# Attention and scan projections of a two-block transformer: fp32 products replaced by three rounded products each, the decay of the keys by one, attention's output projection in two halves

## What is computed

```python
def fox_attention(h, w_in, b_f, g_q, g_k, w_out):        # 16 heads of 64
    q, k, v, f_logit = split(h @ w_in)
    q, k = rms_norm_2(q per head, g_q), rms_norm_2(k per head, g_k)
    cum = cumsum(log_sigmoid(f_logit + b_f))              # per head, over tokens
    s = q @ k.T * 64 ** -0.5 + cum[query] - cum[key]      # causal softmax over keys
    return softmax(mask(s)) @ v @ w_out

def hgrn2_recurrence(h, w_in, b_f, lower_bound, g_o, w_out):   # 8 heads of 128
    q, f_logit, v, g = split(h @ w_in)
    f = lower_bound + (1 - lower_bound) * sigmoid(f_logit + b_f)
    k, q, log_f = 1 - f, silu(q), log(f)
    # per chunk: b = cumsum(log_f)
    # scores[t, s] = sum_k q[t,k] k[s,k] exp(b[t,k] - b[s,k]);  o = scores @ v + (q exp(b)) @ state
    return (rms_norm_2(o, g_o) * silu(g)) @ w_out
```

## Time and profile before

| | us |
|---|---|
| median of 3 runs | 2997.9 |
| lowest and highest | 2996.49 and 3000.87 |
| the profiled execution | 2997.82 |
| its span, first to last instruction | 2996.0 |
| attention stage, first to last job's matmul | about 1428.9 to 1702.9 |
| scan stage, first to last job's matmul | about 2231.0 to 2470.9 |

### The profile page before, as it was taken

One profiled execution on the slowest core, in us unless ns is written; L12 is line 12 of the kernel. 1 busy time (PEld: TensorE's weight loads), 2 busy tenths in 40 slices (PEclk: granted clock), 3 DMA queues, 4 the chain that ended last, 5 costly groups with the idle time before them and its releaser, 6 DMA issues.

```text
span 2996.0 us, 45640 instructions
## 1 busy us (share of the span) xinstructions
PE 2750.9 (92%) x18786; PEld 1951.7 (65%) x18786; DVE 1439.4 (48%) x3248; ACT 777.4 (26%) x1479; POOL 0.2 (0%) x4
## 2 busy tenths in 40 slices
PE   5999887998999997999999999999989989999998
PEld 4998776998999876899766743333346765333332
DVE  3885773787786574654233223333332613333333
ACT  3332352433332253433232111111112332111110
POOL 0000000000000000000000000000000000000000
PEclk9999898999999998999988899999999989999999
DMA  8775420576575420444111169999972124999997
GB/s 341 265 278 228 154 71 32 212 269 235 221 283 202 167 80 7 163 175 183 71 43 57 57 267 427 428 427 428 428 306 98 64 78 186 429 426 427 428 427 300
DMA packets 71735, 701.56 MB, mean 234 GB/s; under 512 B 8672, under 2 KB 11104, under 8 KB 11360
## 3 DMA queue, kind: packets, MB, share of 16 engines
q1 hardware_dynamic: 71520, 698.54, 58.3%
HBM read 697.46 MB, written 1.05 MB: 233 GB/s over the span
## 4 chain that ended last, share of the span: by engine, by line
PE 76%; DVE 10%; DMA 8%; ACT 4%; issue 2%; SPq 0%; DVEq 0%; ACTq 0%
PE ps L790 14%; PE ps L1245 13%; DMA ring<-slabs 7%; PE ps L1266 7%; PE ps L1461 6%; PE ps L1462 6%; PE ps L1463 6%; PE ps L1283 5%; PE ps L783 4%; DVE acc L716 3%; PE ps L1026 2%; PE ps L1413 1%; PE ps L994 1%; PE ps L1215 1%; DVE ring_parts L3005 1%
## 5 line engine op out<-in xcount | busy, mean ns | idle before, releaser
L1461 PE MATMUL ps<-arena_parts 128*128 128x256 f32 x2112 | 606.1, 287 | 24.1 <-DVE arena_parts L3089 24.1
L1462 PE MATMUL ps<-arena_parts 128*128 128x256 f32 x2112 | 601.3, 285 | 0.0
L1463 PE MATMUL ps<-arena_parts,ring_parts 128*128 128x256 f32 x2112 | 601.2, 285 | 0.0
L1245 PE MATMUL ps<-ring,arena 128*64 128x512 f32 x2048 | 470.3, 602 | 5.2 <-ACT arena L1966 4.9
L790 PE MATMUL ps<-h,ring 128*128 128x256 f32 (+1 forms) x1664 | 407.3, 404 | 27.0 <-DVE h L2470 10.0
L1461 PEld LDWEIGHTS ps<-arena_parts 128*128 128x128 f32 x2112 | 409.4, 194 | 25.5 <-issue 25.3
L1462 PEld LDWEIGHTS ps<-arena_parts 128*128 128x128 f32 x2112 | 409.6, 194 | 0.2
L1463 PEld LDWEIGHTS ps<-arena_parts,ring_parts 128*128 128x128 f32 x2112 | 409.1, 194 | 0.0
L790 PEld LDWEIGHTS ps<-h,ring 128*128 128x128 f32 x1664 | 328.6, 200 | 88.3 <-issue 10.9
L3005 DVE TENSOR_TENSOR ring_parts<-ring,arena_parts 128x2048 fp32r<-128x2048 f32 x132 | 299.1, 2288 | 75.7 <-ACT arena_parts L1622 75.7
L1622 ACT CAST arena_parts<-ring 128x2048 fp32r<-128x2048 f32 x132 | 249.4, 1906 | 300.6 <-DMA ring<-slabs 284.4
(11 more groups left out here) (391 smaller groups left out, 2450.3 us busy)
## 6 DMA issues: line engine op xcount, KB each, us to landing
ring<-slabs SPq DMA_DIRECT2D x192, 2048.0 KB, 14.9
ring<-slabs SPq DMA_DIRECT2D x278, 1024.0 KB, 5.0
x<-xT SPq DMA_DIRECT2D x1, 1024.0 KB, 8.8
outT<-x SPq DMA_DIRECT2D x1, 1024.0 KB, 4.7
constants<-const SPq DMA_DIRECT2D x1, 1004.5 KB, 6.6
vectors<-vec SPq DMA_DIRECT2D x1, 747.5 KB, 4.6
ring<-slabs SPq DMA_DIRECT2D x2, 128.0 KB, 3.6
arena<-pos SPq DMA_DIRECT2D x1, 128.0 KB, 7.2
```

What stands on the lines that cost most here:

```text
L1245: mm = nc.tensor.matmul(ps[W * hh:W * hh + W, e % 2, :], xe[:, e % 2, 4 * k + c], wt[:, c], start=(k == 0 and c == 0), stop=(k == 1 and c ...
L1461: nc.tensor.matmul(out, w_hi, v_hi, start=start, stop=False, skip_group_check=True)
L1462: nc.tensor.matmul(out, w_hi, v_lo, start=False, stop=False, skip_group_check=True)
L1463: return nc.tensor.matmul(out, w_lo, v_hi, start=False, stop=stop, skip_group_check=True)
```

## The change

In both stages all projections become three products of float32r (`thirds`). For this each slab is followed in the plan by an entry `high`, which is not loaded but takes a ring slot: ScalarE writes the rounded slab there (`high_part`), VectorE writes the rest over the slab itself (`low_part`). The ring so holds four slabs in place of eight. `h` is split as well, by ScalarE and VectorE, at the entry of each stage and before the output projections. The scan's output norm goes in four pairs of tiles. The cumulated gates of the keys are held as a high and a low part on 48 partitions and added by one float32r product for a head. Half of the attention's output projection (the first four k) runs as 8 `half` jobs within units 18 to 24, each added to `x` at once; the `out` jobs do the other four k. In the scan all value jobs come before the gate jobs.

```diff
 def slab_plan(stages):
-            out += [("foxin", 4 * part + g, "pe") for g in range(4) for part in range(3)]
-            out += [("foxout", s, "pe") for s in range(4)]
+            out += with_low([("foxin", 4 * part + g, "pe") for g in range(4) for part in range(3)]
+                            + [("foxout", s, "pe") for s in range(4)])
+            out += with_low([("hgin", s, "pe") for s in range(16)] + [("hgout", s, "pe") for s in range(4)])
+def with_low(slabs):
+    return [s for one in slabs for s in (one, ("high",) + one[1:])]
-HG_LAST = tuple(range(2, 18, 2)) + (29, 30, 31, 32, 26, 28, 34, 36)
+HG_LAST = tuple(range(2, 18, 2)) + (25, 26, 27, 28, 30, 32, 34, 36)
-            17: ("j27", "t3"), 20: ("t4",), 21: ("t5",)}
+            17: ("j27", "t3"), 18: ("h0", "h1"), 19: ("h2",), 20: ("t4", "h3"), 21: ("t5", "h4"), 22: ("h5",), 23: ("h6",),
+            24: ("h7",)}
+FOX_HIGH = {1: 8, 4: 9, 6: 10, 9: 11, 11: 12, 13: 13, 15: 14, 18: 15}
-        out += value(0) + value(1) + gate(0) + value(2) + gate(4)
+        out += value(0) + value(1) + value(2) + gate(0) + gate(4)
...
 run_jobs, wide jobs (value jobs alike)
+                                mm = thirds(bank(b, n), w_hi[:, k, c0:c0 + P], w_lo[:, k, c0:c0 + P], rhs[0][:, k], v_lo,
+                                            k == ks[0], k == ks[-1])
 attention, scores
-                            mm = nc.tensor.matmul(o, ident[0:FOXH, head:head + 1].to_broadcast([FOXH, qn]),
-                                                  view(NCUM, T2)[0:FOXH, 0:keys], start=False, stop=True)
+                            mm = nc.tensor.matmul(o, part(PICK, FOXH)[64 * e:64 * e + 48, head:head + 1].to_broadcast([48, qn]),
+                                                  part(NCUM, T2)[64 * e:64 * e + 48, 0:keys], start=False, stop=True)
...
 ScalarE
+            def high_part(i):
+                slab_here(act, i)
+                if i + 1 >= RING:
+                    name, value = free[i + 1 - RING]
+                    act.wait_ge(s[name], value)
+                nc.scalar.copy(low_view(i + 1), slab_view(i)).then_inc(s["p_hi"], 1)
 entry of either stage
+                    for j in range(2):
+                        high_part(nth_slab(st, slab, j))
                     norm_root(q, n_norm, n)
+                    for j in range(2, 4):
+                        high_part(nth_slab(st, slab, j))
+                    for k in range(KC):
+                        act.wait_ge(s["h_mul"], n_h + k + 1)
+                        mark(nc.scalar.copy((fox_hi if st[0] == "fox" else sq_parts)[:, k], h[:, k]), q, "h_hi", k)
 attention stage: high(4), fox_forget, high(5), three value_in and root, high(6), fox_keys, root(3), four square, high(7),
 units with high(FOX_HIGH[n_unit]) last in the unit
 scan stage
                 for i in range(16):
                     take(i)
+                    if i >= 3 and i % 2:
+                        high(i // 2 + 3)
 high(11) after the logs; high(12) to high(15) after takes 26, 27, 28, 30; high(16), high(17) before the gate's silu
+                for p in range(4):
+                    await_("act", q, "hon0", 2 * p + 1)
+                    v = sq[:, 2 * p:2 * p + 2]
+                    mark(nc.scalar.activation(v, v, ACT.Exp, scale=-0.5), q, "hon", p)
...
 VectorE
+            def low_part(i):
+                dve.wait_ge(s["p_hi"], halved_at[i] + 1)
+                nc.vector.tensor_tensor(low_view(i), slab_view(i), low_view(i + 1).bitcast(F32), ALU.subtract)\
+                    .then_inc(s["p_lo"], 1)
 entry: low_part of slabs 0 and 1, norm with the subtraction of tile k-2 behind multiply k, low_part of slabs 2 and 3
 attention stage: low parts behind fox_forget, three fox_norm, fox_low_keys, four fox_in (before the first softmax_max)
 scan stage
+                for n in range(4, 8):
+                    low(n)
                 for c in range(KC):
+                    if c in (2, 4, 6):
+                        low(7 + c // 2)
                     dve.wait_ge(s["proj_act"], act_before(q) + KC + c + 1)
 low(11) after the cumulated sums; 12, 13 at the end of tile 1; 14, 15 after levels 1 and 3 of tile 2; 16, 17 at its end
```

More of the change, by code:

```diff
@@ L240, in stage_jobs @@
             out += [("fv", (g, t), 3 * g + 2, 0, "act") for t in range(3)]
+        out += [("half", c, 12 + c // 2, c % 2 * P, "dve") for c in range(KC)]
         out += [("out", c, 12 + c // 2, c % 2 * P, "dve") for c in range(KC)]
@@ L501, in build @@
         split_at = {i: m for m, i in enumerate(split_slabs)}
+        halved = [i for i in range(len(plan) - 1) if plan[i + 1][0] == "high"]
+        halved_at = {i: m for m, i in enumerate(halved)}
         block = ctx.enter_context(nc.Block())
@@ L528, in _ @@
             for i in range(len(plan)):
-                if not (i and paired(plan, i - 1)):
+                if plan[i][0] != "high" and not (i and paired(plan, i - 1)):
                     load(i)
@@ L767, in run_jobs @@
                               "cw": pe_cw}[kind](q, st[1], idx, b)
+                    elif (st[0], kind) == ("fox", "half"):
+                        if idx == 0:
+                            await_("dve", q, "y_lo", 3)
+                        for k in range(4):
+                            mm = thirds(bank(b, n), w_hi[:, k, c0:c0 + P], w_lo[:, k, c0:c0 + P], rhs[0][:, k], rhs[1][:, k],
+                                        k == 0, k == 3)
                     elif kind == "half":
@@ L1133, in hg_scan @@
                         if todo < end:
-                            run_jobs(q, st, todo, todo + 1, slab, job)
+                            run_jobs(q, st, todo, todo + 1, slab, job, rhs=(sq_parts, h_parts))
                             todo += 1
@@ L1579, in _ @@
                             if what == "j":
-                                run_jobs(q, st, i, i + 1, slab, job)
+                                run_jobs(q, st, i, i + 1, slab, job, rhs=ins)
+                            elif what == "h":
+                                run_jobs(q, st, 28 + i, 29 + i, slab, job, rhs=outs)
                             elif what == "s":
@@ L1849, in fox_keys, with hg_act @@
                 await_("pe", q, "ck")
-                mark(nc.scalar.activation(view(NCUM, T2)[0:FOXH], ps[0:FOXH, 2, 0:T2], ACT.Copy, scale=-1.0), q, "ncum")
+                await_("dve", q, "nc0")
+                for at in (0, 64):
+                    ins = nc.scalar.activation(part(NCUM, T2)[at:at + FOXH], ps[0:FOXH, 2, 0:T2], ACT.Copy, scale=-1.0)
+                mark(ins, q, "ncum")
             def fox_output(q, c):
                 await_("pe", q, "y_att", c)
-                mark(nc.scalar.copy(view(FY, KC, T2)[:, c], bank(7, T2)), q, "y_att", c)
-            def hg_act(q, job, st):
+                mark(nc.scalar.copy(h_parts[:, c], bank(7, T2)), q, "y_att", c)
+            def hg_act(q, job, st, slab):
+                high = lambda n: high_part(nth_slab(st, slab, n))
                 hq, hk, hb, hgt = view(HQ, KC, T2), view(HK, KC, T2), view(HB, KC, T2), view(HG, KC, T2)
@@ L2979, in moe_dve, with norm @@
                     sparse_dve(q, l)
-            def norm(n_norm, n_h, n, scale, shift, out, last):
+            def norm(n_norm, n_h, n, scale, shift, out, last, low=None):
                 if last is not None:
@@ L3080, in _ @@
                         split_lo(i)
-                norm(n_norm, n_h, n, scale, shift, out, [written[q]])
+                for j in range(2 if st[0] in HALVED else 0):
+                    low_part(nth_slab(st, slab_at[q], j))
+                low = {"fox": fox_low, "hg": hg_low}[st[0]] if st[0] in HALVED else None
+                norm(n_norm, n_h, n, scale, shift, out, [written[q]], low and (lambda k: low(q, k)))
+                for j in range(2, 4) if st[0] in HALVED else ():
+                    low_part(nth_slab(st, slab_at[q], j))
                 n_norm += 1
```

195 lines of the change are left out of this document (153 added, 42 removed).

## The result

| | before | changed |
|---|---|---|
| median, us | 3001.2 of 6 runs | 2971.8 of 6 runs |
| lowest and highest | 2996.5 and 3012.8 | 2967.1 and 2979.4 |
| the profiled execution | 2997.8 | 2969.7 |
| its span | 2996.0 | 2967.9 |

The changed kernel takes 0.9896 of the time before, 95% interval 0.9880 to 0.9913: 1.0% faster, some 30 us. The forecast was 2978 with a range of 2959 to 3002.

What follows compares the result with a forecast made beforehand. The prediction took TensorE, filled by projection jobs in attention and scan, as the bound. From 2997.8 us, attention's -17.3 (9.5 - 18.5 + 9 - 17.3) and the scan's -2.6 gave 2978; own range 2966 to 2992, overall 2959 to 3002.

Steps and rivals of the forecast that it cites:

- Price of a job: Projection jobs in both stages: 2.98 us wide against 3.68, 3.06 value against 3.65; 53 us gross gain at full clock.
- Rival D: Rounded products miss their rate because weight loads don't hide: wide jobs 4.56 us, 3066 at worst; chance 0.03.
- First turn, +9.5: Attention's entry to first turn: copies and subtractions make it 9.5 us later, savings of 11 jobs included.
- Units to 17, -18.5: Attention units 0 to 17: shorter jobs and decay products save 21.5 us, stalls charged 3, so 18.5 less.
- rival B: Copies and subtractions let ScalarE and VectorE release attention's softmax in seven units: 33 us, not 3, so 3008; chance 0.09.
- the forecast's two bounds: Cost of the seven copies and subtractions in attention's units 0 to 17: 3 us charged, 33 in rival B.
- Tail, +9: Attention's tail: half jobs move in, decay products save 4 to 5; 9 us longer, between -6 and +13.
- rival C: Attention's tail regains full clock, -6 not +9, and 3 us of the entry is hidden: 2960; chance 0.14.
- Output, -17.3: Attention's output projection: 33.7 us becomes 16.4, including 2.9 for the cold start, so 17.3 less.
- Rival A: Shorter jobs make attention run more at 1.2 GHz; units 0 to 17 at 0.75 give 3003; chance 0.12.
- The scan, -2.6: Gated scan stage: job and output savings mostly given back to copies and subtractions; 2.6 us less in sum.
- Expert stages, 0: Expert stages: their first slabs land before the first expert starts, so cost 0.

Runs made afterwards that it cites:

- the first two experiments: Kernel before with fp32 decay product of 48 rows, second head on partitions 64 to 111: 2961.5 us; with 16 rows, second head at 64 to 79: 3000.7 us.
- unit_copies: Changed kernel, attention's slab copies moved ahead of the unit's readings, subtractions one unit later, slabs 6 and 7 into units 0 to 3: 2947.4 us, ratio 0.9817.
- no_halves: Changed kernel without the half jobs, attention's output projection being 8 jobs of 24 products behind attention: 2981.9 us, ratio 0.9940.
- fp32_48_rows_halves: Kernel before with fp32 decay product of 48 rows, plus the half jobs in units 18 to 24, all in fp32: 2949.3 us, ratio 0.9834.
- scan_copies: Changed kernel, scan's subtractions of slabs 10 and 11 moved into the first tile, copies of 16 and 17 into the last tile's levels: 2969.3 us, ratio 0.9888.

## Why the forecast was right, and where it was not

**Sign and size.** 2978 was forecast, 2971.8 measured, inside the forecast's own range of 2966 to 2992. That is closer than the account deserves. The forecast saved 19.9 us from a start of 2997.8; between the medians it was 29.4, from 3001.2. The stage of attention came out at -28.5 for -17.3, outside the 10 to 25 by which the forecast said that it would be wrong; the scan at -3.6 for -2.6. Of attention's four terms one is too small by 4.5, one too large by 13, and one is near only because two errors in it cancel: that the sum stayed in the range is in part luck.

**Price of a job: right.** A wide job takes 3.03 us in a stream (2250.30 to 2253.33 in the scan) for 2.98, its products 0.126 apart for 0.124; a value job's products 0.116 for 0.120. The Trainium skill's N/2.4 + 2.5 ns (TensorE: Matmul & The Clock Gate, Back-to-back issue gap) gives 116 and 109 ns, 8% and 6% below the trace; the page gives it for matmuls without weight loads between them, which the forecast left out, and each product here has one. The timeline of three products:

```profile
2250.30 0.29 PE L763 MATMUL ps<-sq_parts,ring_parts 128*128 128x272 f32 x1
2250.43 0.29 PE L764 MATMUL ps<-h_parts,ring_parts 128*128 128x272 f32 x1
2250.56 0.29 PE L765 MATMUL ps<-sq_parts,ring_parts 128*128 128x272 f32 x1
```

Rival D is refuted. The copy of a slab takes 1.9 and its subtraction 2.29 us, as in the earlier trace rows.

**First turn, +9.5: measured +14.0.** Root (+3.6 for 3.7) and first product (+8.4 for 7.5) are near. Then the logits end 11.8 later for 9.4, and the last job 9.7 for 5.4: that is nearly the whole miss. The terms that are too small are those behind a pause: jobs 2 and 3 waited 2.5 us for VectorE and then took 7.6 us, since their first half ran at the lower clock. The forecast had the wait and no slow products. The copy of slab 6 and the readings behind it gave the wait of 2.45 us before job 9 that the forecast described but did not price, again with slow products behind it. The wait of 4.9 before the first softmax, behind slab 7, came as forecast: it adds 4.3 for the 4.1 in the sum.

**Units to 17, -18.5: measured -20.3, from wrong terms.** The jobs' 10.9 hold by their price. The scores saved 6 x 1.83 + 6 x 1.14 or 1.23 = some 18 us, not 7.9: the step that failed is "Six large and six middle units: 12 x 0.42 + 12 x 0.24 = 7.9", which priced the decay products only and left the score products as they were. They take half the time, since the two heads overlap, and the first two experiments show that this comes from the 48 rows. The stalls were priced at 3; idle time grew by 8.7, and the slower clock took more. That was rival B's mechanism, in part: the forecast took the slack of 5.7 us between exponentials and turn as cover for copy and subtraction, but the subtraction stands ahead of the next softmax, a place whose slack it did not look at. unit_copies shows the price, 18.6 us in the units alone; the cost of B lay between the forecast's two bounds. The two errors nearly cancel in the time, which is luck. (The sums have two slips that change little: 18.8 us at a clock of 0.89 are 21.1, not 21.5, and the scan's tile 1 comes to -0.2, not -0.3.)

**Tail, +9: measured -4.0.** The forecast took the clock at half with the half jobs in. It rose to 0.91, and no_halves and fp32_48_rows_halves show on both sides that the half jobs do it. This is rival C, -6 by its price. The argument from the share of dense work in a unit misled; what spoke for C, that the clock is 0.50 exactly where no job runs, was the stronger row.

**Output, -17.3: measured -18.3.** Right. The start at the lower clock cost less than forecast: the clock was granted at 1.00 up to 1661.0 and at 0.50 for 3.4 us from there, 1.7 us lost for the 2.9 in the sum.

**Rival A**, a lower clock that eats the gain, happened on a small scale (0.85 for 0.88 in the units); with the pauses gone it is 0.94 for the same products, so shorter jobs by themselves did not bring it.

**The scan, -2.6: measured -3.6**, and by the medians 0. Its frame was right: the gain of the first 16 jobs (5.3 us by the time the last one ends, for 4.2) is gone at the second level, which starts 0.6 later than before against the norm's sums (forecast 2.4 later). The profile of before has its first job 1.7 us later than four others with an fp32 scan; against those four the second level is 2.2 later, close to the forecast, and the gain of the jobs 3.6. The output norm starts 2.5 later (3.2), the output projection saves 5.6 (5.4). What the forecast did not see is how little a removed wait is worth there: scan_copies removes 7.3 us of them and gains 0.5, and without any rounded product the scan takes as long.

**Expert stages, 0:** the first took 516.5 to 523.5 us over all profiles, the second 519.0 to 526.1, so a cost of a few us is neither shown nor refuted.

## What to carry to other kernels

Before pricing a change by passes or columns, look at how many rows of the array each product uses and what stands between them: here one edit of row counts (16 to 48, the second head on the upper half) was worth 38 us, and the large rewrite around it gave some of that back. When helper engines prepare operands for TensorE, put copy and subtraction one step apart and behind the work that the next softmax needs, not ahead of it; in these units the pauses cost their length (8 us) and then as much again in slow products (10). Independent dense work belongs in the stretch where the clock is low: here 15 us of it cost 1.7.

## What the runs showed of the hardware

- Two fp32 score products of 64 rows on different halves of the array run at once: their records start 0.01 us apart. With products of 16 rows between them, wherever their rows lie, two heads of 272 keys take 2.61 us (ratio 1.0000), with products of 48 rows 1.12 (0.9867). 32 rows were not tried.
- In the changed kernel the second head's score product starts 0.01 us after the first's, though the first head's decay product is issued between them by the code and starts only 0.36 later. The records don't name their head; that the two are of different heads is read from the 0.33 us between the two records of one head in the kernel before. So matmuls on different rows are not always started in the order of issue, and TensorE's queue is not worked off strictly in order.
- 12 to 15 us of dense products in eight pieces took a stretch of 32 to 37 us from a clock of 0.53 to 0.58 to one of 0.91 to 1.00, in fp32 and rounded form alike.
- The same 15 us or so of TensorE's work cost 3 us in one kernel and 14 in another that differs in where ScalarE and VectorE copy slabs.
